# Moving the weights buffers of a projection kernel to other places modulo 512 bytes

## The chip, the cores and the metric

The kernel runs on one core of a Trainium2 chip. The metric is the device time of one execution in microseconds (us); the kernel before takes 1527.82 us, the median of three runs (1527.73, 1527.82 and 1528.34). Beside the times there is one profiled execution, from which all rows come.

## The reference

The input is x, 1024 rows of 1024 channels in float32. It goes through one decoder block:

```
proj   = x @ w_in                                   # 1024 x 6656 weights
q,k,v,cb,cc,ch,g_conv,g_attn = split(proj)
merged = sigmoid(g_conv) * short_conv(cb, cc, ch)
       + sigmoid(g_attn) * window_attention(q, k, v, sinks)   # 16 heads of 64, 4 kv heads, window 128
x1     = layer_norm(alpha * x + merged @ w_out)     # 1024 x 1024 weights
hid    = silu(x1 @ w_gate) * (x1 @ w_up)            # 1024 x 2816 weights each
out    = layer_norm(alpha * x1 + hid @ w_down)      # 2816 x 1024 weights
```

Everything is float32. Nearly all of the arithmetic is in the five large products.

## The kernel before

Each large product is computed in three passes, because TensorE multiplies a rounded float32 format. Each operand is split into a rounded high part and the low part that is left: x becomes `act_hi` and `act_lo`, a weights tile becomes `w_hi` and `w_lo`. The helper `product` (line 970) then issues, for each 128-deep slice of the contraction, three matmuls of 128x128 weights with 512 moving columns: high weights with high activations (line 975), high weights with low activations (line 976), and low weights with high activations (line 977). Each of these matmuls has its own weights load, which runs beside the matmul before it. So the weights load that runs beside the matmul of line 975 is that of line 976 (high weights), beside line 976 it is that of line 977 (low weights), and beside line 977 it is the next slice's high weights.

The moving operands are `act_hi` and `act_lo` (x, then the normalised x1), the halves `m_hi` and `m_lo` of the merged mixer output (two tensors each), and `hid_hi` and `hid_lo` of the FFN. The weights buffers are `w_hi` and `w_lo` (two slots of 8 slices, filled from `raw`), `w_hi_b` and `w_lo_b` (two slots, filled from `raw_b`), and `wd_hi` and `wd_lo` (two slots for w_down, filled from `raw_d`). ScalarE makes the high part of a tile by a copy (`high_part`, `out_high_part` and `ffn_high_part`, lines 464 to 574 and after), GpSimd makes the low part by a subtraction (lines 379 to 425), and SyncE loads the next tile by one DMA of 512 KB.

The stages follow each other: a prologue that transposes x and projects v and k; a loop over four key heads, each with 12 weights tiles (24 units of 24 matmuls) between which the attention of that head is woven; the output projection (16 units, with `m` moving; slots of `w`, and `wd` for 4 of the units, chosen by `out_slot`); and the FFN in 11 groups of 256 hidden channels. A group has four gate and up tiles, two in `w_b` and two in `w`, each used for two halves of 512 rows, and then 16 short units of six matmuls with `hid` moving and `wd` as weights. The last group computes row by row instead, with `hid` as weights and `wd` moving (lines 1186 to 1191). The order on each engine is written out by hand, and semaphores tie them.

The tensors lie one behind the other in each partition of SBUF in the order of their declarations (lines 108 to 200), and each begins at a multiple of 32 bytes. The first of them, `act_hi`, begins at byte 16512, which is 128 modulo 512. `act_lo`, `res`, `raw`, `w_hi`, `w_lo`, `ident` and `mean_of` are all multiples of 512 bytes long, so all begin at 128 modulo 512. The twelve small tensors from `cw` to `inv2` take 544 bytes, and every large tensor of the later scopes (`q_st`, `pt_hi`, `prob`, `ks_hi`, `vs`, `xs`, `raw_b`, `m_hi`, `m_lo`, `w_hi_b`, `w_lo_b`, `wd_hi`, `wd_lo`, `raw_d`, `hid_hi`, `hid_lo`) begins at 160 modulo 512; `yc` lies at 288. Slices and slots step by multiples of 512 bytes, so a slice begins where its tensor does, modulo 512. Below, the distance of a pair is the place of the weights less the place of the moving operand, modulo 512:

| moving | weights | matmuls | distance before | distance after |
|---|---|---|---|---|
| act | w | 3552 | 0 | hi 64 and 128, lo 192 and 320 (slot 0 and 1) |
| act | w_b | 1056 | 32 | 256 |
| hid | wd | 960 | 0 | 0 |
| m | w | 288 | 480 (32 below) | hi 320 and 384, lo 448 and 64 |
| m | wd | 96 | 0 | 0 |

Of the kernel before, what the change touches and what calls it, by code (L numbers as in the profile page):

```python
# [21 lines left out]
F32R = mybir.dt.float32r  # L22
# [4 lines left out]
P = 128  # L27
D = 1024
S = 1024
DT = D // P  # L30
# [67 lines left out]
def build(nc, x, w_in, conv_w, sinks, w_out, ln1_g, ln1_b, w_gate, w_up, w_down, ln2_g, ln2_b, out):  # L98
    ctx = ExitStack()
    with ctx:  # L100
# [3 lines left out]
        def sb(stack, name, shape, dt=F32):  # L104
            return stack.enter_context(nc.sbuf_tensor(name, shape, dt))


        act_hi = sb(ctx, "act_hi", [P, DT, S], F32R)
        act_lo = sb(ctx, "act_lo", [P, DT, S], F32R)
        res = sb(ctx, "res", [P, DT, S])  # L110
        raw = sb(ctx, "raw", [P, 2, DT, P])
        w_hi = sb(ctx, "w_hi", [P, 2, DT, P], F32R)
        w_lo = sb(ctx, "w_lo", [P, 2, DT, P], F32R)
        ident = sb(ctx, "ident", [P, P])
        mean_of = sb(ctx, "mean_of", [P, P])
        cw = sb(ctx, "cw", [P, DT, 3])
# [8 lines left out]
        neg_mean = sb(ctx, "neg_mean", [P, 2])  # L125
        std2 = sb(ctx, "std2", [P, 2])
        inv2 = sb(ctx, "inv2", [P, 2])


        with ExitStack() as st:  # L130
# [1087 lines left out]
```

## Time and profile before

| what | value |
|---|---|
| device time, median of 3 | 1527.82 us |
| span of the profiled execution | 1526.2 us |
| PE (TensorE matmul) busy | 1503.1 us, 98% |
| PEld (TensorE weights load) busy | 1242.3 us, 81% |
| DVE (VectorE) busy | 697.7 us, 46% |
| ACT (ScalarE) busy | 429.9 us, 28% |
| POOL (GpSimd) busy | 396.0 us, 26% |
| mean granted TensorE clock | 0.994 |
| mean DMA rate | 52 GB/s |

The span goes from the first to the last instruction; the device time holds some 1.6 us more. The recorded end of a matmul is a model and overlaps the next matmul's start, so its duration (about 390 ns) is not what it costs in a stream. What it costs is the distance from its start to the start of the next one, which the timeline shows. DVE, ACT and POOL rows are operations with their durations.

### The profile page before, as it was taken

How to read it: one execution, taken by the hardware profiler on the slowest of the kernel's cores; microseconds unless marked ns; L12 is line 12 of the kernel's file. 1: busy time of each engine (PE TensorE's matmuls, PEld its weight loads, DVE VectorE, ACT ScalarE, POOL GpSimd, SP SyncE). 2: the span in 40 equal slices, each digit the busy share in tenths (PEclk: the TensorE clock that was granted, in tenths of full speed). 3: DMA queues.
4: the chain of work that ended last, by engine and by line, in shares of the span. 5: the costliest groups of instructions: out<-in, count | busy, mean ns of one | idle time of the engine just before them, and what ended most of it. 6: DMA issues, size and time to landing. Idle time of an engine off the chain costs nothing.

```text
span 1526.2 us, 18733 instructions
## 1 busy us (share of the span) xinstructions
PE 1503.1 (98%) x6898; PEld 1242.3 (81%) x6898; DVE 697.7 (46%) x1063; ACT 429.9 (28%) x803; POOL 396.0 (26%) x187
## 2 busy tenths in 40 slices
PE   9999999999999999989989999999999999999997
PEld 8888888888888888868868888888888888888885
DVE  3227662766276637669677231323323132232335
ACT  3423433343334333342443111121112121111223
POOL 2121132113211321136843121302213031221303
PEclk9999999999999999999999999999999999999999
DMA  5111111111111111114332110202101020211002
GB/s 167 56 55 29 43 41 55 29 40 41 55 34 35 41 55 38 31 42 124 89 91 66 44 55 27 82 0 82 55 28 55 27 82 14 69 55 55 0 14 97
DMA packets 127754, 80.07 MB, mean 52 GB/s; under 512 B 7792, under 2 KB 122480, under 8 KB 127728
## 3 DMA queue, kind: packets, MB, share of 16 engines
q1 hardware_dynamic: 127728, 79.73, 17.4%
q8 instruction: 16, 0.26, 0.1%
q14 instruction: 10, 0.08, 0.0%
HBM read 75.53 MB, written 4.19 MB: 52 GB/s over the span
## 4 chain that ended last, share of the span: by engine, by line
PE 96%; DVE 3%; ACT 1%; issue 0%; POOL 0%; ACTq 0%; DVEq 0%; POOLq 0%
PE ps L975 29%; PE ps L977 29%; PE ps L976 29%; PE ps L1084 2%; PE ps L1075 2%; PE ps L1067 1%; PE ps L1066 1%; DVE act_lo L849 0%; DVE m_lo L818 0%; DVE res L868 0%; PE ps L990 0%; DVE bn L938 0%; DVE res L859 0%; DVE raw_d L952 0%; PE ps L998 0%
## 5 line engine op out<-in xcount | busy, mean ns | idle before, releaser
L975 PE MATMUL ps<-act_hi,w_hi 128*128 128x512 f32 x1184 | 463.0, 391 | 1.2 <-DVE act_lo L673 1.2
L977 PE MATMUL ps<-act_hi,w_lo 128*128 128x512 f32 x1184 | 461.7, 390 | 0.0
L976 PE MATMUL ps<-act_lo,w_hi 128*128 128x512 f32 x1184 | 461.4, 390 | 0.0
L381 POOL TENSOR_TENSOR w_lo<-raw,w_hi 128x1024 fp32r<-128x1024 f32 x54 | 131.2, 2430 | 508.4 <-ACT w_hi L468 508.4
L975 PEld LDWEIGHTS ps<-act_hi,w_hi 128*128 128x128 f32 x1184 | 222.4, 188 | 46.7 <-issue 1.4
L977 PEld LDWEIGHTS ps<-act_hi,w_lo 128*128 128x128 f32 x1184 | 222.2, 188 | 46.8
L976 PEld LDWEIGHTS ps<-act_lo,w_hi 128*128 128x128 f32 x1184 | 222.4, 188 | 45.1
L922 DVE TENSOR_TENSOR res<-res,ps 128x512 f32<-128x512 f32 x160 | 109.8, 687 | 94.1 <-PE ps L977 94.1
L401 POOL TENSOR_TENSOR w_lo_b<-raw_b,w_hi_b 128x1024 fp32r<-128x1024 f32 x22 | 52.5, 2408 | 379.2 <-ACT w_hi_b L574 379.2
L975 PE MATMUL ps<-act_hi,w_hi_b 128*128 128x512 f32 x352 | 140.7, 400 | 0.0
L977 PE MATMUL ps<-act_hi,w_lo_b 128*128 128x512 f32 x352 | 139.9, 398 | 0.0
L976 PE MATMUL ps<-act_lo,w_hi_b 128*128 128x512 f32 x352 | 139.9, 397 | 0.0
L975 PE MATMUL ps<-hid_hi,wd_hi 128*128 128x512 f32 x320 | 124.6, 389 | 0.0
L977 PE MATMUL ps<-hid_hi,wd_lo 128*128 128x512 f32 x320 | 124.6, 389 | 0.0
L976 PE MATMUL ps<-hid_lo,wd_hi 128*128 128x512 f32 x320 | 124.5, 389 | 0.0
L900 DVE SCALAR_TENSOR_TENSOR hid<-tanh_g,ps 128x512 f32<-128x512 f32 x44 | 30.3, 688 | 172.5 <-ACT tanh_g L624 172.2
L904 DVE TENSOR_TENSOR hid<-hid,ps 128x512 f32<-128x512 f32 x44 | 30.3, 688 | 164.3 <-PE ps L977 164.0
L626 ACT ACTIVATE hid_hi<-hid 128x512 fp32r<-128x512 f32 x44 | 27.8, 632 | 235.7 <-DVE hid L904 235.7
L401 POOL TENSOR_TENSOR wd_lo<-raw_d,wd_hi 128x1024 fp32r<-128x1024 f32 x22 | 52.6, 2412 | 133.2 <-ACT wd_hi L574 133.2
L975 PEld LDWEIGHTS ps<-act_hi,w_hi_b 128*128 128x128 f32 x352 | 66.7, 189 | 16.5 <-issue 0.5
L976 PEld LDWEIGHTS ps<-act_lo,w_hi_b 128*128 128x128 f32 x352 | 66.6, 189 | 16.6 <-issue 0.5
L977 PEld LDWEIGHTS ps<-act_hi,w_lo_b 128*128 128x128 f32 x352 | 66.5, 189 | 16.2
(144 smaller groups left out, 1919.4 us busy)
## 6 DMA issues: line engine op xcount, KB each, us to landing
raw<-in_w_in SPq DMA_DIRECT2D x52, 512.0 KB, 3.7
raw_d<-in_w_down SPq DMA_DIRECT2D x22, 512.0 KB, 3.3
raw<-in_w_out SPq DMA_DIRECT2D x16, 512.0 KB, 3.6
raw_b<-in_w_gate SPq DMA_DIRECT2D x11, 512.0 KB, 3.8
raw_b<-in_w_up SPq DMA_DIRECT2D x11, 512.0 KB, 4.0
raw<-in_w_gate SPq DMA_DIRECT2D x11, 512.0 KB, 3.9
raw<-in_w_up SPq DMA_DIRECT2D x11, 512.0 KB, 3.9
xs<-in_x SPq DMA_DIRECT2D x8, 512.0 KB, 8.1
```

Source lines behind the costliest of these rows:

```text
L381: pool.tensor_tensor(w_lo[:, slot], raw[:, slot], fp(w_hi[:, slot]), ALU.subtract).then_inc(w_lo_s, 1)
L401: pool.tensor_tensor(ffn_lo(s), ffn_raw(s), fp(ffn_hi(s)), ALU.subtract).then_inc(fw_lo_s, 1)
L626: act.activation(hid_hi[:, t, half(h)], hid[:, t], ACT.Copy, scale=0.5).then_inc(silu_s, 1)
L900: dve.scalar_tensor_tensor(out=hid[:, t], in0=tanh_g[:, t], scalar=1.0, in1=ps[:, 2 * t, :], op0=ALU.add, op1=ALU.mult).then_inc(hid_s, 1)
L904: dve.tensor_tensor(hid[:, t], hid[:, t], ps[:, 2 * t + 1, :], ALU.mult).then_inc(hid_s, 1)
L922: dve.tensor_tensor(res[:, m, half(h)], res[:, m, half(h)], ps[:, 4 + v % 4, :], ALU.add).then_inc(add_s, 1)
L975: pe.matmul(bank, w_h(t), a_hi(t), start=(t == 0), stop=False)
L976: pe.matmul(bank, w_h(t), a_lo(t), start=False, stop=False)
L977: last = pe.matmul(bank, w_l(t), a_hi(t), start=False, stop=(t == tiles - 1))
L1066: pe.matmul(dst, q_st[:, g, blk(n)], ks_hi[:, keys], start=True, stop=False)
L1075: last = pe.transpose(ps[:, TURN + kb, blk(g)], prob[:, g, blk(kb)], ident[:])
L1084: last = pe.matmul(ps[:, OUT, :], vs[:, n - 1 + kb, :], part[:, kb], start=(kb == kbs[0] and part is pt_hi), stop=(kb == 1 and part is pt_lo))
```

## The change

Only places in SBUF change. `w_hi` and `w_lo` are now views into tensors that are 512 bytes longer: `w_hi` begins 64 bytes into its tensor and has 64 more bytes between its two slots, `w_lo` begins 192 bytes into its tensor and has 128 between its slots. An unused tensor `line_up` of 736 bytes behind the small tensors moves all later tensors to 384 modulo 512, that is 256 from `act_hi`. In all 1760 bytes per partition are added. The table above has the distances that follow. `act_hi`, `act_lo`, `res`, `raw`, `ident` and `mean_of` stay where they were modulo 512. No instruction is added, removed or moved to another place in its queue, and no operand changes its shape.

```diff
+        def sb_apart(name, first, between):
+
+            whole = sb(ctx, name, [P, 2 * DT * P + P], F32R)
+            slot = DT * P + between // 4
+            both = whole[:, first // 4:first // 4 + 2 * slot].rearrange("p (s r) -> p s r", s=2)
+            return both[:, :, 0:DT * P].rearrange("p s (t c) -> p s t c", c=P)
...
-        w_hi = sb(ctx, "w_hi", [P, 2, DT, P], F32R)
-        w_lo = sb(ctx, "w_lo", [P, 2, DT, P], F32R)
+        w_hi = sb_apart("w_hi", 64, 64)
+        w_lo = sb_apart("w_lo", 192, 128)
...
         inv2 = sb(ctx, "inv2", [P, 2])
+        sb(ctx, "line_up", [P, 120 + 64])
```

## Rows read from the trace of the kernel before

**Rows 1.** The page: busy time by engine, chain that ended last; waits of PE.
```profile
PE 1503.1 (98%) x6898; PEld 1242.3 (81%) x6898; DVE 697.7 (46%) x1063; ACT 429.9 (28%) x803; POOL 396.0 (26%) x187
PE 96%; DVE 3%; ACT 1%; issue 0%; POOL 0%; ACTq 0%; DVEq 0%; POOLq 0%
...
PE ps L975 <- DVE m_lo L818: 5.3, 3, 2.0
PE ps L1096 <- POOL acc L414: 4.9, 1, 4.9
PE ps L990 <- POOL ident L361: 1.5, 1, 1.5
PE ps L975 <- DVE act_lo L673: 1.2, 1, 1.2
```
**Rows 2.** Groups by form: line, op, out<-moving,weights, xcount | busy us, mean ns | idle before.
```profile
L975 PE MATMUL ps<-act_hi,w_hi 128*128 128x512 f32 x1184 | 463.0, 391 | 1.2 <-DVE act_lo L673 1.2
L975 PE MATMUL ps<-act_hi,w_hi_b 128*128 128x512 f32 x352 | 140.7, 400 | 0.0
L975 PE MATMUL ps<-hid_hi,wd_hi 128*128 128x512 f32 x320 | 124.6, 389 | 0.0
L975 PE MATMUL ps<-m_hi,w_hi 128*128 128x512 f32 x96 | 39.4, 411 | 5.3 <-DVE m_lo L818 5.3
L975 PE MATMUL ps<-m_hi,wd_hi 128*128 128x512 f32 x32 | 12.5, 392 | 0.0
```
**Rows 3.** Timeline of PE, one FFN group: start us, duration us, line, operands.
```profile
1002.56 0.39 PE L975 MATMUL ps<-act_hi,w_hi_b 128*128 128x512 f32 x1
...
1013.76 0.39 PE L975 MATMUL ps<-act_hi,w_hi 128*128 128x512 f32 x1
...
1024.65 0.39 PE L975 MATMUL ps<-hid_hi,wd_hi 128*128 128x512 f32 x1
...
1046.44 0.40 PE L975 MATMUL ps<-act_hi,w_hi_b 128*128 128x512 f32 x1
```
**Rows 4.** Timeline of PE, output projection.
```profile
683.11 0.39 PE L977 MATMUL ps<-m_hi,w_lo 128*128 128x512 f32 x1
...
728.61 0.39 PE L977 MATMUL ps<-m_hi,w_lo 128*128 128x512 f32 x1
...
735.43 0.39 PE L975 MATMUL ps<-m_hi,wd_hi 128*128 128x512 f32 x1
...
745.40 0.39 PE L977 MATMUL ps<-m_hi,wd_lo 128*128 128x512 f32 x1
```
**Rows 5.** Timeline of PE and windows (last row: PE, granted clock, DMA) at half clock.
```profile
781.91 0.63 PE L976 MATMUL ps<-act_lo,w_hi_b 128*128 128x512 f32 x1
...
784.90 0.62 PE L977 MATMUL ps<-act_hi,w_lo_b 128*128 128x512 f32 x1
...
782.00:785.00 3.00, 3.00 (x9) 0.50 0.58 174
```
**Rows 6.** Groups by form: weights loads.
```profile
L975 PEld LDWEIGHTS ps<-act_hi,w_hi 128*128 128x128 f32 x1184 | 222.4, 188 | 46.7 <-issue 1.4
L975 PEld LDWEIGHTS ps<-act_hi,w_hi_b 128*128 128x128 f32 x352 | 66.7, 189 | 16.5 <-issue 0.5
```
**Rows 7.** Groups by form: transposes, whose moving operand is the identity.
```profile
L1075 PE MATMUL ps<-ident,prob 128*128 128x128 f32 x240 | 31.4, 272 | 0.0
L1186 PE MATMUL ps<-ident,res 128*128 128x128 f32 x64 | 9.6, 272 | 0.0
L1006 PE MATMUL ps<-ident,yc 128*128 128x128 f32 x16 | 2.4, 272 | 0.0
```
**Rows 8.** Groups by form: ScalarE and GpSimd on the weights buffers.
```profile
L574 ACT ACTIVATE wd_hi<-raw_d 128x1024 fp32r<-128x1024 f32 x22 | 22.1, 1051 | 165.5 <-PE ps L977 165.5
L574 ACT ACTIVATE w_hi_b<-raw_b 128x1024 fp32r<-128x1024 f32 x22 | 22.0, 1045 | 0.0
L574 ACT ACTIVATE w_hi<-raw 128x1024 fp32r<-128x1024 f32 x22 | 21.9, 1044 | 0.0
L401 POOL TENSOR_TENSOR w_lo_b<-raw_b,w_hi_b 128x1024 fp32r<-128x1024 f32 x22 | 52.5, 2408 | 379.2 <-ACT w_hi_b L574 379.2
L401 POOL TENSOR_TENSOR w_lo<-raw,w_hi 128x1024 fp32r<-128x1024 f32 x22 | 52.3, 2399 | 3.0 <-ACT w_hi L574 3.0
```

## The prediction

> **What bounds the kernel now.** I read the page first, then the waits of TensorE, then the groups by form, and last the timeline, where the matter is decided. The page has TensorE busy for 98% of the span and on 96% of the chain that ended last [rows 1]. Its waits for other engines are small: 5.3, 4.9, 1.5 and 1.2 us, 12.9 in all [rows 1]. So this kernel costs what its stream of matmuls costs, and 1 ns more or less on each of the 5952 matmuls of `product` is 6.0 us of device time with nothing to hide it.
>
> What does one such matmul cost? The recorded durations are all near 390 ns, but they hold a modelled end that overlaps the next one. Yet they already split: matmuls of one shape have a mean of 391 ns with weights in `w`, 389 in `wd` and 400 in `w_b` [rows 2]. The starts give the price itself. In one FFN group the 48 matmuls with `w_b` run from 1002.56 to 1013.76, which is 11.20 / 48 = 233.3 ns each; the 48 with `w` from 1013.76 to 1024.65, 10.89 / 48 = 226.9; the 96 of `hid` with `wd` from 1024.65 to 1046.44, 21.79 / 96 = 227.0 [rows 3]. In the output projection, 195 steps of `m` with `w` take 728.61 - 683.11 = 45.50 us, 233.3 each, and 44 steps of `m` with `wd` take 745.40 - 735.43 = 9.97 us, 226.6 each [rows 4].
>
> Set beside the distances of the pairs, this is a pattern. Distance 0 costs 226.6 to 227.0 ns in three pairs (act with w, hid with wd, m with wd), distance 32 and distance 480, which is 32 on the other side, cost 233.3 in two (act with w_b, m with w). It isn't the absolute place: `wd` lies at 160 modulo 512 and is cheap, `w_b` lies at 160 too and is dear; `w` is cheap with `act` and dear with `m`. So relative place matters, by 6.5 ns in 227, and no other difference of these pairs (shape, queue, waits) explains it.
>
> A second reading tells how much there is to win. In a stretch of half the clock (granted 0.50) the same pair act with w_b takes (784.90 - 781.91) / 7 = 427 ns [rows 5]. That is 512 columns at 1.2 GHz (426.7 ns) with nothing over. At 2.4 GHz 512 columns are 213.3 ns, so at full clock distance 0 pays 13.5 ns over the columns and distance 32 pays 20.0. As the excess is gone at half clock, it isn't a fixed cost of an instruction in the array; it looks like two reads of SBUF, the moving operand and the next weights, that get in each other's way only at full speed. The loads themselves last 188 and 189 ns, no longer where the matmul is slower [rows 6], so it is the moving operand that gives way.
>
> **The change part by part.** Instructions, their order, waits and DMAs stay the same, so only speeds can differ.
>
> *The later tensors at 384 instead of 160.* 1056 matmuls of act with w_b go from distance 32 to 256. No row shows distance 256. Bounds: as before (233.3), or down to the bare columns, 213.3, a gain of 21 us; above, another 6.6 ns on top as the step from 0 to 32 was, 7 us lost. I take distance 0's price, 226.7, as the nearest row that fits a period of 64, 128 or 256 bytes: gain 1056 x 6.6 ns = 7.0 us. hid with wd and m with wd stay at 0: nothing.
>
> *w at 64, 128 (high) and 192, 320 (low) from act.* 3552 matmuls leave distance 0, and this is the part that decides. One third runs beside a load of each of: low weights (line 976), the same high weights (line 975), the next high weights (line 977). So two thirds of these matmuls see 64 or 128 and one third 192 or 320. No row shows any of them. Bounds: 213.3 ns, the bare columns, a gain of 3552 x 13.4 = 48 us; and 233.3, the only price of a distance other than 0 that I have, a loss of 3552 x 6.5 = 23 us. Transposes with weights at 0, 32 and 160 from the identity all have 272 ns [rows 7], so 160 is not worse than 0 there, but with 128 columns the matmul is shorter than its load and a conflict could hide. The symmetry of +32 and -32 speaks for a period of which 32 is half, that is 64 bytes: then all the new distances are multiples of the period and cost what 0 costs. I take that, 226.7 ns, no change; the value is the nearest to the rows, and it lies between the two ends.
>
> *m with w.* 288 matmuls go from 480 to 320, 384, 448 and 64, all multiples of 64. Same choice: 288 x 6.6 = 1.9 us gained; ends -5.8 and +1.9 us.
>
> *The rest.* Where a stream passes from one pair to another (act to vs and prob in the attention, w to w_b and wd) some 150 matmuls see 32 before and a multiple of 64 after; at 6.6 ns this is up to 1.0 us, of which I take 0.6. The copies and subtractions on the weights buffers read and write the same contiguous 1024 elements: 1044, 1045 and 1051 ns on ScalarE and 2399 and 2408 on GpSimd at either of the two places [rows 8], so places make no difference there, and both engines are busy for 28% and 26% of the span only. A TensorE that is faster by 1% asks for its weights 1% earlier, which those engines can give.
>
> The sum against the profiled execution: 1526.2 - 7.0 - 1.9 - 0.6 = 1516.7 us of span. The median of the runs shown is 1.6 us above that span (1527.8), so 1518.3 us.
>
> **What the notes say.** Two rules of the Trainium skill speak against any effect. "SBUF — State Buffer", section "Who interferes with whom", says that TensorE and ScalarE never wait on anyone, and "TensorE: Matmul & The Clock Gate", section "Step-by-step: what each phase is for", that the moving operand and the weights have two independent read ports, so that loading the next weights takes no bandwidth from the running matmul. By them the time would stay at 1527.8. The trace doesn't agree: 233.3 against 226.9 ns for the same shape under the same load [rows 3], and none of the excess at half clock [rows 5].
>
> **The rivals.**
>
> *A, forecast, period of 64 bytes:* 1518.3 us, own range 1516 to 1521. For it: +32 and -32 cost the same, and all three pairs at 0 agree.
>
> *B, the excess is an overlap of two reads that distance removes.* Then 0 and 32 are both near, and some of 64 to 320 are free of it. If half of the 3552 lose their 13.4 ns, this gives 24 us beside A's 9.5: 1494 us; if all do and w_b as well, 1527.8 - 47.6 - 21.1 - 5.8 = 1453. For it: the excess of 13.4 ns at distance 0 vanishes at half clock, so it can be avoided in principle. Against it: the first step away from 0 made it larger, on both sides.
>
> *C, slower: distance 0 is the one good place,* since both reads start together and keep in step, and any other is like 32. The mechanism acts on act with w in the in-projection and the FFN: 3552 x 6.6 ns = 23.4 us more, w_b and m stay dear: 1551.3 us. It decides as soon as more than 1344 of the 3552 (what w_b and m can give back at best) pay the 6.6 ns. For it: every nonzero distance in the trace is dear. Against it: there is only one nonzero size.
>
> *D, slower or about even: a period of 128 or 256 bytes,* with 0 and 256 cheap. At 128, distances 64, 192 and 320 are dear and 128 is cheap: high slot 0 (1184 matmuls) and both low slots (1184) pay 6.6 ns, 15.6 us more, less 7.0 for w_b and about 0.6: 1536. At 256 all four are dear: 1551 less 7.0 = 1544.
>
> *E, no change:* placement doesn't do what the rows suggest, or the parts cancel: 1527.8.
>
> **How the numbers follow.** Chances: A 0.34, B 0.20, C 0.15, D 0.21, E 0.10. The likeliest is A, 1518.3. The range should leave out 2 in 10: from 1489, which holds A and the half of B in which at most half of the matmuls gain, to 1552, which holds D and C at their prices. The ends that go further are B complete and a distance dearer than 32. This measurement can tell about 0.2% (3 us) from no change. Faster by more: A and B, 0.54, and a little of D where high slot 1 is cheaper than before, 0.56. Slower by more: C and most of D, 0.34. Within: 0.10.
>
> **What would show it right or wrong.** In the timeline of one FFN group, the steps with w_b should be 226.7 ns and no longer 233.3 (the group about 0.64 us shorter than its 65.99), those with hid and wd unchanged at 227.0, those with w unchanged at 226.9, in both slots alike. In the output projection, m with w should fall to 226.7. If the starts with w differ by slot, the period is longer than 64 bytes (D), and the two slots tell which distance is cheap; if both rise to 233, C is right; if any falls under 224, B. If w_b stays at 233.3 at distance 256, the period doesn't divide 256 or there is none. The prediction is wrong as a whole if the loads get longer than 189 ns or if TensorE waits more than its 12.9 us for others.

## The result and the profile after

The changed kernel takes 1533.6 us (median of 5 runs, 1533.2 to 1534.0) against 1527.7 us for the kernel before in the same session: a ratio of 1.0038 with a 95% interval from 1.0025 to 1.0050. It is slower by 5.9 us where 9.5 us less was forecast. The time lies inside the stated range, on the wrong side of no change.

The page of the changed kernel has the same instructions and nearly the same shares as before [rows 1]: busy time and chain by engine, then TensorE's two largest waits.

```profile
PE 1507.8 (98%) x6898; PEld 1241.4 (81%) x6898; DVE 698.1 (46%) x1063; ACT 429.9 (28%) x803; POOL 397.4 (26%) x187
PE 95%; DVE 3%; ACT 1%; issue 0%; POOL 0%; ACTq 0%; DVEq 0%; POOLq 0%
...
PE ps L982 <- DVE m_lo L825: 5.3, 3, 2.0
PE ps L1103 <- POOL acc L421: 5.1, 1, 5.1
```

All of TensorE's waits come to 13.7 us against 12.9 before, so some 5 of the 5.9 us must lie in the matmuls' own steps. The groups by form of the changed kernel (line 982 is line 975 of before) show it in the mean durations already, beside [rows 2]: w went from 391 to 395 ns, w_b from 400 to 392, wd stayed at 389.

```profile
L982 PE MATMUL ps<-act_hi,w_hi 128*128 128x512 f32 x1184 | 467.4, 395 | 1.1 <-DVE act_lo L680 1.1
L982 PE MATMUL ps<-act_hi,w_hi_b 128*128 128x512 f32 x352 | 138.0, 392 | 0.0
L982 PE MATMUL ps<-hid_hi,wd_hi 128*128 128x512 f32 x320 | 124.5, 389 | 0.0
L982 PE MATMUL ps<-m_hi,w_hi 128*128 128x512 f32 x96 | 39.2, 408 | 5.3 <-DVE m_lo L825 5.3
```

The price is again the distance from start to start. The timeline of the changed kernel: two rows that bound 215 matmuls of the prologue and the first unit of the head loop, then one FFN group.

```profile
46.22 0.39 PE L983 MATMUL ps<-act_lo,w_hi 128*128 128x512 f32 x1
...
95.66 0.39 PE L984 MATMUL ps<-act_hi,w_lo 128*128 128x512 f32 x1
...
922.46 0.39 PE L982 MATMUL ps<-act_hi,w_hi_b 128*128 128x512 f32 x1
...
933.34 0.40 PE L982 MATMUL ps<-act_hi,w_hi 128*128 128x512 f32 x1
...
938.91 0.39 PE L982 MATMUL ps<-act_hi,w_hi 128*128 128x512 f32 x1
...
944.42 0.39 PE L982 MATMUL ps<-act_hi,w_hi_b 128*128 128x512 f32 x1
...
966.40 0.39 PE L982 MATMUL ps<-hid_hi,wd_hi 128*128 128x512 f32 x1
...
988.17 0.39 PE L982 MATMUL ps<-act_hi,w_hi_b 128*128 128x512 f32 x1
```

The 48 with w_b take 10.88 us, 226.7 ns each (233.3 in [rows 3]). The 48 with w take 11.08 us, 230.8 each (226.9 before): the 24 of slot 0, at distance 64 and 192, 5.57 us or 232.1 each, the 24 of slot 1, at 128 and 320, 5.51 us or 229.6. The 96 of hid with wd take 21.77 us, 226.8. In the prologue 214 steps with w take 49.44 us, 231.0 each.

Summed over all steps of the two traces, act with w costs 14.6 us more, act with w_b 7.9 less, m with w 0.6 less, hid with wd 0.1 less and all else 0.4 less: together the 5.5 us by which the spans differ (1531.7 and 1526.2). In 1.6 us of the first two only the clock moved: a stretch of half clock that lay on matmuls with w_b before [rows 5] is split in two now, and the second half lies on matmuls with w. The windows of the changed kernel show that piece (columns as in [rows 5]); the length of half clock ahead of the last rows is the same in both runs, 10.2 us.

```profile
800.50:803.50 3.00, 3.00 (x9) 0.50 0.00 0
```

### The profile page after: what moved, and what is told of

Its sections match the earlier page's. It is cut to its first block, busy times and chain, and to the rows that moved or that the text cites. A ratio compares the mean times of both kernels' runs of the same rounds, so it can differ in the third digit from the quotient of the medians.

```text
span 1531.7 us, 18733 instructions
## 1 busy us (share of the span) xinstructions
PE 1507.8 (98%) x6898; PEld 1241.4 (81%) x6898; DVE 698.1 (46%) x1063; ACT 429.9 (28%) x803; POOL 397.4 (26%) x187
## 4 chain that ended last, share of the span: by engine, by line
PE 95%; DVE 3%; ACT 1%; issue 0%; POOL 0%; ACTq 0%; DVEq 0%; POOLq 0%
PE ps L982 29%; PE ps L984 29%; PE ps L983 29%; PE ps L1091 2%; PE ps L1082 2%; PE ps L1074 1%; PE ps L1073 1%; DVE act_lo L856 0%; DVE m_lo L825 0%; DVE res L875 0%; DVE bn L945 0%; PE ps L997 0%; DVE res L866 0%; DVE raw_d L959 0%; PE ps L1005 0%
## 5 line engine op out<-in xcount | busy, mean ns | idle before, releaser
L984 PE MATMUL ps<-act_hi,w_lo 128*128 128x512 f32 x1184 | 467.0, 394 | 0.0
L633 ACT ACTIVATE hid_hi<-hid 128x512 fp32r<-128x512 f32 x44 | 27.8, 632 | 233.9 <-DVE hid L911 233.9
```

The lines of the kernel that those rows point to most:

```text
L633: act.activation(hid_hi[:, t, half(h)], hid[:, t], ACT.Copy, scale=0.5).then_inc(silu_s, 1)
L984: last = pe.matmul(bank, w_l(t), a_hi(t), start=False, stop=(t == tiles - 1))
```

## The experiments

Each run below changes places alone, unless it is said otherwise. Most use this helper, which starts the first slot `first` bytes into a tensor that is 512 bytes longer and puts `between` bytes between the slots:

```diff
+        def sb_at(stack, name, first, between, inner):
+            whole = sb(stack, name, [P, 2 * D + P], F32R)
+            slot = D + between // 4
+            both = whole[:, first // 4:first // 4 + 2 * slot].rearrange("p (s r) -> p s r", s=2)[:, :, 0:D]
+            return both.rearrange("p s (t c) -> p s t c", c=P) if inner else both
```

In the diffs below, pairs of lines that say the same for high and low are set as one. Where w_b and wd are moved, two unused tensors of 1024 bytes between the `m` tensors keep the overlays as they were.

**Each half of the change alone.** First the later tensors at 256, w back at 0:

```diff
         inv2 = sb(ctx, "inv2", [P, 2])
+        sb(ctx, "line_up", [P, 56])
```

> w_hi and w_lo are back at distance 0 from act; all later tensors stay 256 from act (w_b at 256, m with w at 256, hid with wd and m with wd at 0). Theory 1 (price set by the distance modulo 256, cheapest at 0): all five pairs take 226.7 ns per matmul, and the time is that of before less 1344 x 6.6 ns = 8.9 us, about 1518 us. Theory 2 (any multiple of 64 that stays the same from matmul to matmul is cheap; what costs is the change of distance between high and low weights): the same, 1518 us. If neither place matters by itself (noise of layout), 1528.

Measured: 1517.65 us, a ratio of 0.9933 (0.9919 to 0.9946), with a span of 1515.7. Its timeline, one FFN group:

```profile
932.11 0.39 PE L983 MATMUL ps<-act_hi,w_hi_b 128*128 128x512 f32 x1
...
942.99 0.39 PE L983 MATMUL ps<-act_hi,w_hi 128*128 128x512 f32 x1
...
953.87 0.39 PE L983 MATMUL ps<-hid_hi,wd_hi 128*128 128x512 f32 x1
...
975.63 0.39 PE L983 MATMUL ps<-act_hi,w_hi_b 128*128 128x512 f32 x1
```

10.88, 10.88 and 21.76 us are 226.7 ns for all three pairs. So 256 is as good as 0, and this version is faster than both kernels, by 10.0 us than the one before and by 15.9 than the changed one.

Then the other half, w moved as in the change and the later tensors where they were:

```diff
-        sb(ctx, "line_up", [P, 120 + 64])
```

> The changed kernel without line_up: w stays at 64, 128, 192 and 320, the later tensors go back to 160 modulo 512 (w_b at 32, m with w at 32, 96, 160 and 288). Theory 1: w_b back at 233.3 ns, w unchanged at 230.7, so the changed kernel's time plus 1056 x 6.6 = 7.0 us and up to 0.8 us for m with w: about 1541 us. If the two parts aren't additive, something other than the matmuls' own price is at work.

Measured: 1540.7 us, ratio 1.0089 (1.0072 to 1.0106). Over the settled steps (all but the first six and the last of a stretch) w_b costs 233.3 ns and w 230.75, in the changed kernel 226.7 and 230.74. The halves give +12.9 and -10.0 us, 2.9 together where the change has 5.9. That 3 us isn't in the settled steps of w and w_b, which agree to 0.1 ns; the first six steps of a stretch with w take 229.9 ns on average before, 228.7 with only the later tensors moved and 232.1 with only w moved, but 231.8 with both changes, which is 0.5 us more than the parts give. m with w gained 1.5 us in the run with only the later tensors moved and 0.6 in the change; its distance is 256 in the one and 320, 384, 448 and 64 in the other, so here the parts can't add up. Two other things met that stage in the run with w back at 0: TensorE waited less for `m_lo` than its 5.3 us, and another 3.4 us ran at half the clock, which cost about 1.6 us (the wait, then a window with columns as in [rows 5]):

```profile
PE ps L983 <- DVE m_lo L826: 3.8, 2, 2.0
...
672.60:675.60 3.00, 3.00 (x8) 0.50 0.01 3
```

At equal clock the parts would give even less together, so the 3 us isn't the clock. The rest of it I can't place.

**One distance for high and low weights and both slots.**

```diff
+        w_hi, w_lo     = sb_at(ctx, ..., 64, 0, True)     # act with w at 64
+        w_hi_b, w_lo_b = sb_at(st, ..., 96, 0, True)      # act with w_b at 128
+        wd_hi, wd_lo   = sb_at(st, ..., 192, 0, False)    # hid with wd at 192
```

> High and low weights and both slots at one distance per pair: act with w at 64, act with w_b at 128, hid with wd at 192. Theory 1 (distance modulo 256 sets the price): w about 232 ns, w_b about 230, wd about 232, time about 1543 us. Theory 2 (only a change of distance between matmuls costs, multiples of 64 are cheap): all three 226.7 ns, time about 1521 us.

Measured: 1549.3 us, ratio 1.0143 (1.0127 to 1.0158). Timeline of one group: w_b, w, wd, and the next w_b.

```profile
950.43 0.39 PE L986 MATMUL ps<-act_hi,w_hi_b 128*128 128x512 f32 x1
...
961.59 0.40 PE L986 MATMUL ps<-act_hi,w_hi 128*128 128x512 f32 x1
...
972.79 0.40 PE L986 MATMUL ps<-hid_hi,wd_hi 128*128 128x512 f32 x1
...
994.77 0.39 PE L986 MATMUL ps<-act_hi,w_hi_b 128*128 128x512 f32 x1
```

232.5 ns at 128, 233.3 at 64 and 229.0 at 192. A constant distance doesn't help, so theory 2 and with it the period of 64 fall; theory 1's own guesses miss by 1.3 to 3 ns. The same with 320 for w (first 320), 96 for w_b (first 64) and 160 for wd (first 160):

> High and low weights and both slots at one distance per pair: act with w at 320, act with w_b at 96, hid with wd at 160. Theory 1 (period 256): w costs at 320 what it costs at 64 in the run that has w at 64, to 0.3 ns; w_b at 96 and wd at 160 somewhere from 229 to 235. Theory 2 (period 64): w 226.7, w_b and wd 233.3 as at 32, time about 1534 us.

Measured: 1555.8 us, ratio 1.0181 (1.0165 to 1.0196).

```profile
954.34 0.39 PE L986 MATMUL ps<-act_hi,w_hi_b 128*128 128x512 f32 x1
...
965.58 0.39 PE L986 MATMUL ps<-act_hi,w_hi 128*128 128x512 f32 x1
...
976.77 0.39 PE L986 MATMUL ps<-hid_hi,wd_hi 128*128 128x512 f32 x1
...
999.17 0.39 PE L986 MATMUL ps<-act_hi,w_hi_b 128*128 128x512 f32 x1
```

234.2 ns at 96, 233.1 at 320 and 233.3 at 160. Over the settled steps of the whole trace 320 costs 233.34 and 64 cost 233.35: with 0 and 256 alike too, the period is 256 bytes. Then nearer places, 16 for w, 8 for w_b and 240 (16 below) for wd:

> Constant distances nearer than 32: act with w at 16, act with w_b at 8, hid with wd at 240 (16 below). Theory 1 (distance 0 modulo 256 is a single good place; two streams of reads at a fixed relation of places): all three above 227 and up to 233.3, with 16 and 240 alike. Rival (the price follows which 32-byte block the two begin in): 16 and 8 cost 226.7 as distance 0 does, and only 240 is dear. A place that is better than 0 would show as a mean under 226 ns.

```profile
947.30 0.40 PE L986 MATMUL ps<-act_hi,w_hi_b 128*128 128x512 f32 x1
...
958.38 0.39 PE L986 MATMUL ps<-act_hi,w_hi 128*128 128x512 f32 x1
...
969.58 0.40 PE L986 MATMUL ps<-hid_hi,wd_hi 128*128 128x512 f32 x1
...
991.51 0.39 PE L986 MATMUL ps<-act_hi,w_hi_b 128*128 128x512 f32 x1
```

Measured (one execution, 1543.1 us): 230.8 ns at 8, 233.3 at 16, 228.4 at 240. Neither of the two forecasts is right in full: there are no blocks of 32 bytes, and 16 and 240 aren't alike. And 4 for w, 248 for w_b, 224 for wd:

> Constant distances: act with w at 4, act with w_b at 248 (8 below), hid with wd at 224 (32 below, modulo 256). Theory 1 (period 256): wd 233.3, as m with w at 480 before; w at 4 and w_b at 248 between 226.7 and 233.3. Rival (blocks of 32 bytes): w 226.7, w_b 233.3.

```profile
948.25 0.40 PE L986 MATMUL ps<-act_hi,w_hi_b 128*128 128x512 f32 x1
...
959.46 0.39 PE L986 MATMUL ps<-act_hi,w_hi 128*128 128x512 f32 x1
...
970.60 0.39 PE L986 MATMUL ps<-hid_hi,wd_hi 128*128 128x512 f32 x1
...
993.00 0.39 PE L986 MATMUL ps<-act_hi,w_hi_b 128*128 128x512 f32 x1
```

Measured (one execution, 1549.0 us): 232.3 ns at 4, 233.3 at 248 and 233.35 at 224, over the settled steps, as theory 1 had it. At 4 bytes, a single column, 5.6 ns of the 6.6 are lost already. All settled prices of a constant distance together:

| distance mod 256 | 0 | 4 | 8 | 16 | 32 | 64 | 96 | 128 | 160 | 192 | 224 | 240 | 248 |
|---|---|---|---|---|---|---|---|---|---|---|---|---|---|
| ns | 226.7 | 232.3 | 230.6 | 232.6 | 233.3 | 233.3 | 234.3 | 232.4 | 233.4 | 228.9 | 233.3 | 228.3 | 233.3 |

Place 0 has the lowest mean of the thirteen. The table takes most places from one pair, but where another pair had the same distance the price agrees: 96 cost 234.3 ns in m with w too, 128 cost 232.5 in m with wd (both in the run with weights at 128 further down), and 240 cost 228.7 in m with w and 227.5 in m with wd.

These are means, and single steps differ even at a constant distance, in patterns that repeat. At 32 (act with w_b before) they alternate between 235 and 232 ns; at 192 they take 232, 226 and 229 ns in the order of the three matmuls of a slice; at 128 they lie between 228 and 241. So a single step can be as cheap as at place 0, and what a step costs isn't settled by its own distance.

**High and low weights at different distances,** both slots alike: w high 0 and low 128, w_b high 256 and low 0, wd high 128 and low 0.

```diff
+        w_hi = sb_at(ctx, "w_hi", 0, 0, True);   w_lo = sb_at(ctx, "w_lo", 128, 0, True)
+        w_hi_b = sb_at(st, "w_hi_b", 224, 0, True);   w_lo_b = sb_at(st, "w_lo_b", 480, 0, True)
+        wd_hi = sb_at(st, "wd_hi", 128, 0, False);   wd_lo = sb_at(st, "wd_lo", 0, 0, False)
```

> High weights and low weights at different distances, both slots alike: act with w high 0 and low 128; act with w_b high 256 and low 0; hid with wd high 128 and low 0. Theory 1 (price by the distance modulo 256 of the next weights, matmul by matmul): w_b 226.7 ns throughout; w 226.7 on the steps beside a load of high weights and about 230 on those beside a load of low weights (mean 228); wd the reverse (mean 229). Theory 2 (a change of distance costs): w_b above 229 although both its distances are multiples of 256.

```profile
947.39 0.39 PE L986 MATMUL ps<-act_hi,w_hi_b 128*128 128x512 f32 x1
...
958.27 0.39 PE L986 MATMUL ps<-act_hi,w_hi 128*128 128x512 f32 x1
...
969.37 0.39 PE L986 MATMUL ps<-hid_hi,wd_hi 128*128 128x512 f32 x1
...
991.75 0.40 PE L986 MATMUL ps<-act_hi,w_hi_b 128*128 128x512 f32 x1
```

Measured (one execution, 1541.9 us): w_b 226.7 ns although its distance jumps by 256 at each low part, so a change by the period is free. But w costs 231.3 where 228 was expected, and wd 233.1 where 229 was. By line the settled steps of w are 227.7, 232.6 and 233.9 ns: the third step, whose load is at distance 0 again, is dearer than the one with the load at 128. So the price of a step isn't given by the distance of its own load alone; what came before it counts. Hence the changed kernel's slot 1 (128 and 320) can be cheaper, at 229.6, than either of its distances kept constant (232.4 and 233.3), which no sum over single distances gives.

**What the excess is.** With w at 0 and the later tensors at 256, the moving operand of act with w_b reads one column 512 times over, and the loads of wd read one column 128 times over.

```diff
+            def one_column(ap, n):
+                return ap[:, 0:1].broadcast_to([P, n])
```

> The layout with w at 0 and all later tensors at 256, but the matmuls with w_b read one moving column 512 times over, and the loads of wd read one column of weights 128 times over; the sums of gate, up and down are other ones than the reference's. If the excess over 213.3 ns comes from the moving reads and the load's reads meeting as both sweep through the same places, both pairs fall to about 216 ns or less (w stays 226.7, time about 1518 - 2016 x 11 ns = 1496 us). Rival (a fixed cost of the rounded format or of a load at full clock): both stay at 226.7 and the time at 1518 us. If only w_b falls, it is the moving sweep; if only wd, the load's sweep.

```profile
931.67 0.38 PE L983 MATMUL ps<-act_hi,w_hi_b 128*128 128x512 f32 x1
...
942.03 0.39 PE L983 MATMUL ps<-act_hi,w_hi 128*128 128x512 f32 x1
...
952.92 0.40 PE L983 MATMUL ps<-hid_hi,wd_hi 128*128 128x512 f32 x1
...
975.11 0.38 PE L983 MATMUL ps<-act_hi,w_hi_b 128*128 128x512 f32 x1
```

Measured (one execution, 1512.0 us): a moving operand that stays in place costs 215.8 ns: of the 13.4 ns over the columns that distance 0 pays, 10.9 come from the moving operand's walk through SBUF, and 2.5 are left. So a fixed cost of the format is out. But loads that stay in place make it 231.1, dearer than the 226.7 of loads that walk along. So only half of the first forecast came in. At half clock (granted 0.50) the difference is gone: in this same execution act with w_b, which stays, and m with w, which walks, both take 427 ns a step.

The next run reads the 512 columns in alternating runs, from the first and the second 1024 bytes, so that the moving reads pass the places modulo 256 at half the pace. Runs of 4 columns for w, 16 for w_b and 8 for wd, all weights at 128. The columns are written to PSUM in the same broken order.

```diff
+            def woven(ap, run):
+                return ap.rearrange("p (b l c) -> p l b c", b=2, c=run)
```

> The 512 moving columns are read (and written to PSUM) in another order: a run of columns from the first 1024 bytes, then the same run from the second, so the moving reads go through the places modulo 256 at half the pace, which is the pace of a load that takes 128 columns in the 107 ns that a transpose's step shows. Runs of 4 columns for w, 16 for w_b, 8 for wd; all weights at distance 128. Theory 1 (meetings of two sweeps cost the excess): side by side at 128 apart the sweeps never meet and the pairs fall to about 216 ns, for at least the finer runs: time about 1527.8 - 5568 x 11 ns = 1467 us at best. Rival (the excess belongs to any moving read of changing places): 227 ns or more; if a jump between runs costs by itself, the pair with runs of 4 is dearest.

```profile
932.56 0.41 PE L986 MATMUL ps<-act_hi,w_hi_b 128*128 128x512 f32 x1
...
944.08 0.41 PE L986 MATMUL ps<-act_hi,w_hi 128*128 128x512 f32 x1
...
956.07 0.41 PE L986 MATMUL ps<-hid_hi,wd_hi 128*128 128x512 f32 x1
...
979.43 0.40 PE L986 MATMUL ps<-act_hi,w_hi_b 128*128 128x512 f32 x1
```

Measured (one execution): 1631.1 us, with 240.0 ns for runs of 16, 243.3 for runs of 8 and 249.8 for runs of 4. The forecast of 216 ns is refuted. How much of this belongs to the reads and how much to the broken order of the writes this run doesn't tell. The same with all weights at distance 0:

> The same orders of moving columns, with all weights at distance 0. Theory 1: the two sweeps now go together in the same places, so the price is well above that of distance 128 with the same order, above 233 ns for some pair. Rival (order alone or distance alone sets the price): the same as at distance 128.

Measured (one execution): 1632.4 us and 240.0, 243.3 and 250.2 ns, the same as at 128 to 0.4 ns. With a walk broken in this way the difference between 0 and 128 doesn't act. Last, with the layout of the fastest version, short walks again and again. In one run the moving operand of both pairs repeats its first 32 columns, and the load reads one column, 8 in w_b and 40 in wd:

```diff
+            def again(ap, start, cols, n):
+                one = ap[:, start:start + cols].rearrange("p (o c) -> p o c", o=1)
+                return one.broadcast_to([P, n // cols, cols])
```

> Layout of the run with w back at 0. In the pairs with w_b and with wd the moving operand reads its first 32 columns (128 bytes) 16 times over; the load reads one column 128 times over, in w_b column 8 (inside the same 128 bytes modulo 256), in wd column 40 (in the other 128 bytes). Gate, up and down are other sums than the reference's. Theory 1 (meetings in the same place modulo 256 cost the excess): wd about 216 ns plus what the 15 jumps back cost, w_b clearly above wd, by 5 ns or more. Rival (the load's place doesn't act, only the moving operand's own walk does): w_b and wd the same within 0.5 ns.

```profile
936.89 0.40 PE L983 MATMUL ps<-act_hi,w_hi_b 128*128 128x512 f32 x1
...
948.20 0.40 PE L983 MATMUL ps<-act_hi,w_hi 128*128 128x512 f32 x1
...
959.09 0.40 PE L983 MATMUL ps<-hid_hi,wd_hi 128*128 128x512 f32 x1
...
981.71 0.40 PE L983 MATMUL ps<-act_hi,w_hi_b 128*128 128x512 f32 x1
```

Measured (one execution, 1537.0 us): 235.6 ns in both, the rival's case. Where the load sits doesn't act here. And the PSUM writes are in plain order here, so a broken order of reads costs time by itself. In the other run loads are as they are, and w_b repeats 32 columns, wd 64 columns (256 bytes):

> Layout of the run with w back at 0, loads as they are (128 columns). With w_b the moving operand reads its first 32 columns 16 times over, with wd its first 64 columns (256 bytes) 8 times over; gate, up and down are other sums than the reference's. Theory 1 (only the place modulo 256 counts): wd costs what the plain walk costs at distance 0, 226.7 ns, as it passes the same places modulo 256; w_b, which stays in half of the places, meets the load in another rhythm, between 216 and 240. Rival (a jump costs by itself, as the runs of 4, 8 and 16 columns suggest at 0.7 to 0.8 ns per jump): wd about 226.7 + 7 x 0.8 = 232 ns.

```profile
934.23 0.40 PE L983 MATMUL ps<-act_hi,w_hi_b 128*128 128x512 f32 x1
...
945.59 0.40 PE L983 MATMUL ps<-act_hi,w_hi 128*128 128x512 f32 x1
...
956.51 0.39 PE L983 MATMUL ps<-hid_hi,wd_hi 128*128 128x512 f32 x1
...
978.27 0.40 PE L983 MATMUL ps<-act_hi,w_hi_b 128*128 128x512 f32 x1
```

Measured (one execution, 1528.6 us): wd 226.7 ns, as the plain walk, and w_b 236.7. A jump back by 256 bytes is free, one by 128 bytes is not. This fits the period of 256 bytes a second time, now on the moving side. The rival fails, and its 0.7 to 0.8 ns per jump wasn't a constant before either: over the 215.8 ns of an operand that stays, the 31 jumps of runs of 16 cost 0.78 ns each, the 63 and 127 jumps of runs of 8 and 4 only 0.44 and 0.27.

## Why the prediction was wrong

The reading of the kernel before held. The time is the stream of matmuls, the relative place of weights and moving operand sets 6.6 ns of each step, no other engine mattered (the copies stayed at 1044 to 1052 ns, the loads at 188), and each half of the sum that didn't rest on w came in: w_b at 256 fell from 233.3 to 226.7 ns, hid with wd and m with wd stayed. With w left alone the time is 1517.65 us, where the sum had 1518.3. That it fits to 0.7 us is in part luck: 1.5 us less waiting for `m_lo` and 1.6 us more of half clock, neither of them in the sum, nearly cancel. One of the prediction's signs of being wrong as a whole was met in the changed kernel, where TensorE waits 13.7 us and not 12.9, but 0.8 us doesn't carry the result.

The step that failed is the one that the text named as the one that decides: "I take that, 226.7 ns, no change" for the 3552 matmuls of act with w. It rested on the equal price of +32 and -32, read as a period of 64 bytes. Two points on either side of a good place can't tell a short period from a single good place. The text called 226.7 the value nearest to the rows, but both rows of a distance other than 0 had 233.3, and this upper bound was the truth for a constant 64 or 320. The settled steps came out 4.0 ns dearer. Summed directly, the pair cost 14.6 us more, of which 1.6 are the clock, so the term was 13.0 us in place of 0. With the forecast's -7.0 for w_b and the measured -0.6 for m with w this gives 1527.8 + 5.4 = 1533.2; measured 1533.6.

m with w was mis-sized by the same step: 0.6 us gained instead of 1.9, at 230.8 ns in place of 226.7, since its new distances (320, 384, 448 and 64) aren't multiples of 256 either.

Of the rivals, D names the mechanism: a period of 256 bytes with all four new distances dear. Its 1544 us was too high since it took 6.6 ns for each; the mixed distances of high and low weights cost 4.0 on average. C, "distance 0 is the one good place", is nearly right about the places and wrong only about 256. B's hope that distance frees a step of its excess is refuted for the means of all twelve other places.

The two rules of the Trainium skill that the prediction names ("SBUF — State Buffer", section "Who interferes with whom", and "TensorE: Matmul & The Clock Gate", section "Step-by-step: what each phase is for") would have no change at all; the run with w at 0 and w_b at 256 is faster by 0.7% through places alone, so the measurement decides against them here.

What stays open is the machinery. A walking moving operand costs 10.9 ns over one that stays, and nothing at half clock, where both take 427 ns; the price has a period of 256 bytes on the side of the weights, and the moving side fits it; its mean is lowest when the load starts at the moving operand's place, and it depends on the steps before. But the picture of two reads that meet in one place, on which B stood, isn't borne out, in two ways: broken walks cost the same at distance 0 and 128, and a load held inside or outside the places that the moving operand reads costs the same.

## What to carry to other kernels

When matmuls of one shape have two mean durations in the groups by form, take the step from start to start for each pair of operands and set it beside their addresses; here small tensors whose sizes add up to 32 bytes over a multiple of 512 stood in front of the weights and cost 10 us of 1528, and 224 bytes of padding gave them back. For steps like these (512 moving columns of this format, a weights load beside each) align weights and moving operands to the same place modulo 256 bytes, all of them, and don't take a place that no row shows for a good one because it is a round number. When the term that decides the sign has no row, leave the forecast's sign open: the bounds went from 48 us gained to 23 us lost, and here even their middle would have been a gain. A change that keeps the good pair where it is and moves only the dear one needs no such term; it was the fastest run here.

## What the runs showed that was not expected

A matmul of 512 columns in this format takes 215.8 ns when its moving operand stays in place, 226.7 when it walks with the next weights at its own place modulo 256, and 228 to 234 elsewhere; a shift of 4 bytes is enough for 232.3. Moving operands that are read (and written to PSUM) in runs of 16, 8 and 4 columns from two places cost 240.0, 243.3 and 250 ns, at distance 0 and 128 alike. After a change from distance 32 to 0 the steps need about six matmuls to settle: in the 21 stretches of the kernel before in which w follows w_b, the first six take 228.9 ns on average and the later ones 226.7, while with w_b at 256 the first six take 226.6.
